# First attention of a two-block transformer kernel: the transposes of the probabilities issued as products with the identity

## The reference

```python
s = jnp.einsum('bqhd,bkhd->bhqk', qb, k).astype(jnp.float32) * scale
s = s + cq[..., None] - cum[:, :, None, :]
p = jax.nn.softmax(jnp.where(pos[None, :] <= tq[:, None], s, MASK_VALUE), axis=-1)
return jnp.einsum('bhqk,bkhd->bqhd', p.astype(v.dtype), v)
```

## Time and profile before

| | us |
|---|---|
| median of 3 runs | 2596.1 |
| lowest and highest run | 2588.16 and 2601.82 |
| the profiled execution | 2601.68 |
| its span, first to last instruction | 2599.9 |
| mean granted TensorE clock over the span | 0.981 |
| TensorE busy | 2520.6 (97%) |
| VectorE busy | 1568.6 (60%) |
| ScalarE busy | 1025.7 (39%) |

### The profile page before, as it was taken

One profiled execution on the slowest core, in us unless ns is written; L12 is line 12 of the kernel. 1 busy time (PEld: TensorE's weight loads), 2 busy tenths in 40 slices (PEclk: granted clock), 3 DMA queues, 4 the chain that ended last, 5 costly groups with the idle time before them and its releaser, 6 DMA issues.

```text
span 2599.9 us, 35147 instructions
## 1 busy us (share of the span) xinstructions
PE 2520.6 (97%) x15126; PEld 2030.0 (78%) x15126; DVE 1568.6 (60%) x1843; ACT 1025.7 (39%) x1246; POOL 88.1 (3%) x162
## 2 busy tenths in 40 slices
PE   6999999889899999999999899999999999999999
PEld 3479997767688888888888788887888777777887
DVE  6778884666755555555444665546954454446864
ACT  2033334445443333333333444543654333333332
POOL 0000000000000000000000000001000000000000
PEclk9999999789899999999999999999999999999999
DMA  9988995333366666655555654456655333335654
GB/s 409 427 303 315 349 359 208 123 129 132 135 225 223 229 222 226 226 213 208 179 193 194 251 184 147 177 206 213 226 185 188 125 125 121 127 131 219 253 184 162
DMA packets 77802, 549.44 MB, mean 211 GB/s; under 512 B 8807, under 2 KB 8967, under 8 KB 22737
## 3 DMA queue, kind: packets, MB, share of 16 engines
q1 hardware_dynamic: 56656, 405.36, 43.2%
q0 software_dynamic: 20992, 141.85, 14.4%
HBM read 531.46 MB, written 12.58 MB: 209 GB/s over the span
## 4 chain that ended last, share of the span: by engine, by line
PE 90%; DVE 5%; DMA 3%; ACT 1%; issue 1%; SPq 0%; DVEq 0%; ACTq 0%
PE psum L2138 40%; PE psum L1015 25%; PE psum L2153 7%; PE psum L2211 4%; PE psum L2371 2%; PE psum L2121 2%; DMA weights<-in_loads 1%; DMA xT<-in_loads 1%; PE psum L1143 1%; PE psum L1152 1%; PE psum L1150 1%; PE psum L2193 1%; PE psum L2290 1%; PE psum L2312 1%; DVE arena L2577 1%
## 5 line engine op out<-in xcount | busy, mean ns | idle before, releaser
L1828 ACT ACTIVATE unit_high<-weights 128x1024 fp32r<-128x1024 f32 (+1 forms) x501 | 717.6, 1448 | 1098.7 <-PE psum L2138 612.9
L2533 DVE TENSOR_TENSOR unit_low<-weights,unit_high 128x2048 fp32r<-128x2048 f32 x229 | 524.6, 2291 | 441.3 <-ACT unit_high L1828 440.9
L1388 DVE TENSOR_TENSOR unit_low<-weights,unit_high 128x1024 fp32r<-128x1024 f32 x240 | 289.2, 1221 | 188.8 <-ACT unit_high L1828 188.7
L2138 PE MATMUL psum<-unit_high,z_high 128*128 128x512 f32 x1152 | 290.7, 395 | 1.8 <-DVE arena L2870 1.8
L2138 PE MATMUL psum<-unit_high,z_low 128*128 128x512 f32 x1152 | 284.7, 389 | 0.0
L2138 PE MATMUL psum<-unit_low,z_high 128*128 128x512 f32 x1152 | 284.6, 389 | 0.0
L1015 PE MATMUL psum<-unit_high,z_high 128*128 128x512 f32 x960 | 284.6, 406 | 0.0
L1015 PE MATMUL psum<-unit_high,z_low 128*128 128x512 f32 x960 | 266.9, 394 | 0.0
L1015 PE MATMUL psum<-unit_low,z_high 128*128 128x512 f32 x960 | 263.8, 396 | 1.3 <-DVE unit_low L1388 1.3
L2138 PEld LDWEIGHTS psum<-unit_high,z_high 128*128 128x128 f32 x1152 | 215.8, 190 | 46.4 <-DVE arena L2870 2.2
L2138 PEld LDWEIGHTS psum<-unit_high,z_low 128*128 128x128 f32 x1152 | 216.2, 188 | 45.3
(11 more groups left out here) (405 smaller groups left out, 2817.0 us busy)
## 6 DMA issues: line engine op xcount, KB each, us to landing
weights<-in_loads SPq DMA_DIRECT2D x380, 1024.0 KB, 4.8
arena<-in_ada_early POOLq DMA_DIRECT2D x26, 2048.0 KB, 11.3
xn<-in_loads POOLq DMA_DIRECT2D x44, 512.0 KB, 5.3
weights<-in_ada_early POOLq DMA_DIRECT2D x8, 2048.0 KB, 21.3
xT<-in_loads POOLq DMA_DIRECT2D x12, 512.0 KB, 3.9
gates_kept<-h POOLq DMA_DIRECT2D x12, 512.0 KB, 3.5
arena<-gates_kept POOLq DMA_DIRECT2D x12, 512.0 KB, 8.5
arena<-in_b_rows POOLq DMA_DIRECT2D x10, 512.0 KB, 6.9
```

The costliest lines, as they stand in the source:

```text
L1388: ins = V.tensor_tensor(ring_lo[:, g % RING, c], ring[:, g % RING, c], unit_hi[:, g % 2, c].bitcast(F32), ALU.subtract)
L1828: return nc.scalar.activation(out_, in_, ACT.Copy, scale=scale)
L2138: ins = mm(psum[:, bank + m, 0:width], xk[:, m * P:(m + 1) * P], w[:, k, 0:width], start=(first and i % 8 in (0, 4) and part == 0), stop=( ...
L2533: V.tensor_tensor(ring_lo[:, g % RING], ring[:, g % RING], unit_hi[:, g % 2].bitcast(F32), ALU.subtract)\
```

## The change

The operands, the target in PSUM, the order and all waits stay. The call is another: a matmul with the probabilities as stationary side (`lhsT`) and the identity as moving side, in an accumulation group of its own, in place of the transpose call, which takes the same two operands in the same roles.

```diff
                 for j in range(2):
                     for a in range(0, nk, P):
                         w = min(P, nk - a)
-                        ins = nc.tensor.transpose(psum[0:w, TRB, j * SEQ + a:j * SEQ + a + P],
-                                                  prob[:, n % 2, j, a:a + w], ident)
+                        ins = nc.tensor.matmul(psum[0:w, TRB, j * SEQ + a:j * SEQ + a + P],
+                                               prob[:, n % 2, j, a:a + w], ident, start=True, stop=True)
                 ins.then_inc(s_["pt_sum"], 1)
```

## The result

| | before | after |
|---|---|---|
| median of 20 runs each | 2596.18 us | 2604.14 us |
| lowest and highest | 2588.16, 2607.33 | 2598.82, 2613.57 |
| profiled execution | 2601.68 us | 2598.99 us |

The ratio of the times is 1.0031, 95% interval 1.0018 to 1.0044: the changed kernel is slower by 8 us, less than the 0.5% that I had set as what a measurement can tell with ease, but clear of no change over 20 runs. I had predicted 2605 us. Which mechanism gave that number is another question: two of its terms were off in opposite directions.

A forecast was written before the change was run, and what follows sets the result against it. The prediction took TensorE, busy for 97% of the span, as the bound. Work 17.6 plus half-rate surcharge 3.5, less 5 hidden and 7 of clock, gave +9 us: median 2605 us, range 2592 to 2616 (8 times in 10).

The forecast's parts named there:

- The price of one: At L2312, each plain f32 product costs two 0.11 us records, a transpose one; with weight loads 17.6 us more at full rate.
- The bound of 46 us: Upper bound of the added work at L2312, if a product took four times a transpose; kernel then near 2640 us.
- What is hidden: Score products' 9 waits for VectorE, 13.8 us in sum, swallow 5 us of the added work; bounds 0 and 13.8.
- The clock: Denser thin places in the stage win back 7 of 27.8 us not granted; bounds -5 and 27.8.
- Surcharge: Some 35 of the 136 added records run at half rate, each about 0.10 us dearer: 3.5 us.
- The sum: Whole kernel: 17.6 + 3.5 - 5 - 7 = +9 us, median 2605 us; chance 0.45.
- signs of being wrong: Wrong if L2312 has 136 records, a record takes over 0.13 us, or stage clock is 0.95 or more or under 0.85.
- two thin places: Half-rate stretches follow TensorE's waits and the steps whose scores add products over 7 of 128 rows (L2296, L2298).
- Nothing softens the price: Rival: clock pattern stays and waits for pieces keep their length; +16 to +21 us, 2612 to 2617; chance 0.25.
- The clock comes back: Rival: thin places no longer drop the clock in the half-rate stretches; -8 us, 2588; chance 0.13.
- The price is hidden: Rival: the score products' waits absorb all of their 13.8 us; 0 to +7 us, 2596 to 2603; chance 0.14.
- The change doesn't do what it says: Rival: the product at L2312 leaves one record like the transpose; time stays at 2596 us; chance 0.03.

The follow-up runs named there:

- products in those steps alone: Kernel before with products for transposes only in the 8 steps of the forgetting heads (24 of 136): 2599.9 us, ratio 1.0011.
- products in all the one-block steps: Kernel before with products for transposes only in the 28 steps with one block of keys (56 of 136): 2603.8 us, ratio 1.0024.
- those in all the two-block steps: Kernel before with products for transposes only in the 20 steps with two blocks of keys (80 of 136): 2604.5 us, ratio 1.0022.
- the kernel with one thin product less: Kernel before without the first of two 7-row products per head in the forgetting heads' scores: 2581.0 us, ratio 0.9940; with products for transposes 2592.2.
- leaving out both: Kernel before without both 7-row products per head in the forgetting heads' scores, so without the forget term: 2577.2 us, ratio 0.9919.
- small pieces: Kernel before with 24 modulation-weight pieces cut from 512 to 16 columns in fetch and accumulation: 2579.8 us with transposes, 2583.8 with products.
- 544: Changed kernel with every product issued twice into the same place, 544 records in L2312: 2618.9 us, ratio 1.0085 to the kernel before.

## Why the prediction was right

*The price of one.* Right. One more record per transpose, 0.11 us at full rate, and 272 records. Over the steps that ran at full rate in the two traces, one of four transposes is 0.50 us longer (0.50 worked out) and one of two 0.26 (0.27 worked out), so 17.4 us for 20 and 28 such steps where 17.6 was predicted. The bound of 46 us, and with it the rule that the transpose mode is four times faster for FP32 (the Trainium skill, TensorE: Matmul & The Clock Gate, Terms), is out: the factor is two in these traces.

*What is hidden.* By the means mis-sized, and not settled. I took 5 us, so 12.6 us of the work should have been left, and the full-rate times leave 16.5 ± 0.6: about 1 us hidden. The traces say more. TensorE's idle time in the stage falls by 3.9 us in this pair, by 3.8 without waits for pieces, and the scores' wait is 4.5 us shorter. One pair of executions, whose full-rate times scatter by 2 us each, doesn't decide it; between 1 and 4 us are hidden, and the 5 is too much by either.

*The clock.* Mis-sized the other way. Surcharge and return together were put at 3.5 - 7 = -3.5 us; the clock loss fell by 8.7 ± 1.4 (about 8 if half rate costs what the traces show). The surcharge alone is near what was taken: an added record costs 0.24 us at half rate ((1.86 - 0.91) / 4) where 0.21 was worked out, so the return is the term that was too small.

*The sum.* That it came out is luck. By the means, 4 us too much was taken as hidden and 5 us too little as returned; the two errors cancelled, and so +9 met +7.8. And one of my own signs of being wrong came true: I had named a stage clock of 0.95 or more, and the profiled execution has 0.97 and a stage 5.2 us shorter, where I had expected 0.89 to 0.91 and 9 us longer. That execution is a favourable one (5.1 us under its median). But the loss outside the stage is (1 - 0.981) x 2599.9 - 27.8 = 22 us in the trace before and (1 - 0.987) x 2597.3 - 6.4 = 27 in this one. That leaves 12 to 17 of the mean 38.7 us for the stage, an estimate of 0.92 to 0.94. So my clock was too low for the mean execution as well, and not only for this one.

*What gives the clock back.* Half right. That transposes count as work, read from the earlier trace rows, is confirmed by the run with the transposes issued twice, and the rule that they don't (the Trainium skill, TensorE: Matmul & The Clock Gate, Part 4: PE-mode transpose) does not hold here: their clock loss is 36.0 us against 47.4. Of the two thin places that I named, the waits for pieces are not needed: with these waits down to 3.2 us the return is as large or larger (14.8 ± 3.3). The forgetting steps are tied to it, since with one of their thin products gone the loss falls by 13.5 us and the change's return vanishes. But products in those steps alone bring nothing that can be told, nor do products in all the one-block steps, and those in all the two-block steps bring 2.9 us. Why all steps together bring back more than their parts is open, and with it where the return comes from. That thin work as such drops the clock is argued from the kernel with one thin product less; leaving out both did not lower the loss further.

*The rivals.* "Nothing softens the price" (2612 to 2617) had the price nearly right and missed the clock. "The clock comes back" would have needed 25 us of return; the profiled execution of the changed kernel looks like it (27.8 - 6.4 = 21.4 us in the stage) and is 5 us under its median, so from that one profile this rival would have seemed confirmed. "The price is hidden" is out by the full-rate time (+16.5) and by the 16.8 us that TensorE still stands idle. "The change doesn't do what it says" is out by the 272 records.

## What to carry to other kernels

A plain f32 product with the identity (128x128) costs two records where a transpose costs one; where TensorE is the bound, keep the transpose. Where executions of one kernel differ by more than the change, split each time into granted clock and the rest before asking where it went: here that took the standard deviation of one kernel's executions from 4.7 to 1.9 us. When two traces are compared, cut the windows by the same work, not by the same microseconds. And where the clock falls while TensorE is busy without a gap, look for thin products to leave out before adding denser ones: the term that the softmax removes anyway was worth 16 us here, twice the change in the other direction. Leaving out the second one too did not lower the clock loss further (37.8 against 34.0).

## What the runs showed of the hardware that was not expected

The spread of the kernel's times is mostly the clock's. The loss over an execution is 47.4 us in the mean before, and the same program's executions range from a mean granted clock of 0.978 to 0.984.

More work for TensorE in all steps at once lowers the clock loss: 47.4 us with 136 records in L2312, 36.0 to 38.7 with 272, 28.8 with 544. Of the 41.3 us that the largest added, 18.6 came back. With small pieces the same step from 136 to 272 records gave back 14.8 ± 3.3 of 17.5 us. It doesn't hold for every addition: products in the one-block steps alone (192 records) left the loss at 49.2 ± 1.7, those in the forgetting steps alone (160 records) at 47.0 ± 1.6, and on top of the kernel without the first thin product the change left it at 33.5, from 34.0.
